# Two feed-forwards of a two-block network: up projections as seven block products instead of eight, down projections in one group per tile

## The reference

```python
def _swiglu(x, w1, w3, w2):
    return (jax.nn.silu(x @ w1) * (x @ w3)) @ w2
...
        x = _layernorm(DEEPNORM_ALPHA * x + 0.5 * _swiglu(x, ffn1_w1[l], ffn1_w3[l], ffn1_w2[l]),
                       ln1_g[l], ln1_b[l])
...
        x = _layernorm(DEEPNORM_ALPHA * x + 0.5 * _swiglu(x, ffn2_w1[l], ffn2_w3[l], ffn2_w2[l]),
                       ln3_g[l], ln3_b[l])
```

## Time and profile before

| | us |
|---|---|
| median of 3 runs | 3948.86 |
| lowest, highest | 3948.81, 3955.92 |
| profiled execution, span from first to last instruction | 3945.0 |
| TensorE busy | 3484.9 (88%) |
| VectorE busy | 1899.4 (48%) |
| ScalarE busy | 1151.9 (29%) |
| GpSimd busy | 80.0 (2%) |

### The profile page before, as it was taken

The page is one execution under the profiler, slowest core; times in us unless marked ns, Lnnn a source line. Parts: engine busy times, 40 slices in busy tenths (PEclk is TensorE's granted clock), DMA queues, the critical chain, the costliest instruction groups (busy, mean ns, idle before and its releaser), DMA issues. The chain is left out here.

```text
span 3945.0 us, 67598 instructions
## 1 busy us (share of the span) xinstructions
PE 3484.9 (88%) x30402; PEld 2794.9 (71%) x30402; DVE 1899.4 (48%) x2705; ACT 1151.9 (29%) x1713; POOL 80.0 (2%) x91
## 2 busy tenths in 40 slices
PE   2999899999757777779999999989967989999997
PEld 1888677887246767747888888767645768888885
DVE  7565455642656656446222222467785552222226
ACT  2111232222534334333211111235565331111113
POOL 0000000000000000000000000020000020000000
PEclk9999899999779999979999999999968999999999
DMA  4233311231741331142111111221000211111112
...
DMA packets 141692, 284.70 MB, mean 72 GB/s; under 512 B 8156, under 2 KB 81004, under 8 KB 141148
## 3 DMA queue, kind: packets, MB, share of 16 engines
...
...
## 5 line engine op out<-in xcount | busy, mean ns | idle before, releaser
L242 DVE TENSOR_TENSOR ring_b_wl<-ring_b_raw,ring_b_wh 128x1024 fp32r<-128x1024 f32 (+1 forms) x200 | 236.5, 1183 | 1112.9 <-ACT ring_b_wh L239 1112.9
L274 PE MATMUL PS<-ffn_x_high,ring_b_wh 128*128 128x512 f32 x1408 | 551.0, 391 | 13.1 <-DVE ffn_x_low L537 9.5
L239 ACT ACTIVATE ring_b_wh<-ring_b_raw 128x1024 fp32r<-128x1024 f32 (+1 forms) x200 | 204.6, 1024 | 1181.3 <-PE PS L276 1169.5
L276 PE MATMUL PS<-ffn_x_high,ring_b_wl 128*128 128x512 f32 x1408 | 549.2, 390 | 0.0
L275 PE MATMUL PS<-ffn_x_low,ring_b_wh 128*128 128x512 f32 x1408 | 549.0, 390 | 0.0
L274 PEld LDWEIGHTS PS<-ffn_x_high,ring_b_wh 128*128 128x128 f32 x1408 | 265.2, 188 | 73.8 <-issue 9.5
L276 PEld LDWEIGHTS PS<-ffn_x_high,ring_b_wl 128*128 128x128 f32 x1408 | 265.0, 188 | 55.3
L275 PEld LDWEIGHTS PS<-ffn_x_low,ring_b_wh 128*128 128x128 f32 x1408 | 265.2, 188 | 54.9 <-issue 0.2
L274 PE MATMUL PS<-ffn_hid_high,ring_b_wh 128*128 128x512 f32 x704 | 275.1, 391 | 2.6 <-DVE ring_b_wl L242 2.6
L276 PE MATMUL PS<-ffn_hid_high,ring_b_wl 128*128 128x512 f32 x704 | 273.9, 389 | 0.0
L275 PE MATMUL PS<-ffn_hid_low,ring_b_wh 128*128 128x512 f32 x704 | 273.9, 389 | 0.0
...
## 6 DMA issues: line engine op xcount, KB each, us to landing
...
```

What stands on the lines that cost most here:

```text
L239: return nc.scalar.activation(out, x, ACT.Copy)
L242: return nc.vector.tensor_tensor(out, x, high.bitcast(fp32), ALU.subtract)
L274: nc.tensor.matmul(out, wh, xh, start=k == 0, stop=False)
L276: last = nc.tensor.matmul(out, wl, xh, start=False, stop=k == kt - 1)
```

## The change

Only `ffn_stage` and the helpers it needs are rewritten. Hidden tiles 0 and 1 stay plain products (`plain`), 4 tiles x 2 token halves. For each hidden tile q = 2 to 21 (the code's quads), the two up tiles, each split into halves of k, form a 2x2 block matrix A (A11, A12 from w1, A21, A22 from w3), and `x` split by k and by tokens forms B (B11, B12, B21, B22). The four result blocks come of seven products of 4 blocks of k x 3 matmuls, on sums of blocks:

- On the weights, made by GpSimd for every q (`sums`): S1 = A21 + A22, S2 = S1 - A11, S3 = A11 - A21 (in place of A21), S4 = A12 - S2.
- On the data, made once: T1 and T2 by VectorE, T3 and T4 by GpSimd.
- The products in order: A11 B11, S2 T2, S1 T1, S3 T3, A12 B21, A22 T4, S4 B22. Each fills one of PSUM's banks 0 to 3. ScalarE copies the first to scratch; VectorE adds the others up in seven additions (`combine`), and two multiplications (`gate`) follow on ScalarE's two Silus, now from SBUF.

Both parts of every one of the seven operands are cut anew (128x512 each), into four slots of high parts and eleven slots that hold raw blocks, sums and, in place, their low parts. VectorE may overwrite A11 with its low part only after GpSimd's third sum, which still reads A11 (`SUMS_FOR`).

The down projection no longer sums over pieces. After the seven products of q all eight row tiles (down blocks) of hidden tile q - 2 follow: 6 matmuls each over 1024 tokens, in banks 4 and 5 or 6 and 7 by turns, and each added to `xT` at once by VectorE (`update`). A block may start when the update two before it is done. At q = 20 and 21 only the first token half is done so; the rest of it (hidden tiles 20 and 21 for the first half, 18 to 21 for the second) is left to the tail, in four single banks. The bias that `ffn2` adds to `xT` moves from GpSimd to ScalarE, as eight instructions of 128x1024 between the cuts of q = 2. Down weights come as one tile of a hidden tile's 1024 outputs.

```diff
-            PIECES = [(0, 8), (8, 8), (16, 6)]
-            tiles = []
-            for p, (first, n_hid) in enumerate(PIECES):
-                both = [("down", p, m, (0, 1)) for m in range(KD)]
-                if p == len(PIECES) - 1:
-                    both = [("down", p, m, (c,)) for c in range(2) for m in range(KD)]
-                tiles += [("up", p, m, (0, 1)) for m in range(2 * n_hid)] + both
...
+            KH = KD // 2
+            N_PLAIN = 2
+            QUADS = range(N_PLAIN, KF)
+            B11, B21, T1, T2, T3, T4, B22 = range(7)
+            PRODUCTS = (("A11", B11), ("S2", T2), ("S1", T1), ("S3", T3), ("A12", B21), ("A22", T4), ("S4", B22))
+            BANK_READ = ((-1, 2), (-1, 5), (-1, 6), (-1, 7), None, (0, 1), (0, 4))
+            PLACE = {w: i for i, (w, *_) in enumerate(PRODUCTS)}
+            ALLOC = ("A11", "S3", "A12", "A22", "S1", "S2", "S4")
+            BLOCKS = {"A11": (0, 0), "A12": (0, KH), "S3": (1, 0), "A22": (1, KH)}
+            SUMS_FOR = {"A11": 3, "S2": 4, "S1": 2, "S3": 3, "A12": 4, "A22": 1, "S4": 4}
...
+            BLOCKS_AFTER = {q: (0, 0, 0, 0, 0, 0, KD) for q in QUADS}
+            LOW_ORDER = (B11, B21, None, B22, T2, T1, T3, T4)
...
+                def await_slot(eng, q, w):
+                    j = allocation(q, w)
+                    if j >= N_SLOTS:
+                        was = j - N_SLOTS
+                        eng.wait_ge(prod.h, prod.base + number(N_PLAIN + was // 7, PLACE[ALLOC[was % 7]]) + 1)
+                    elif j >= 7:
+                        eng.wait_ge(prod.h, prod.base + 4 + (j - 7) // 2 + 1)
+                    elif j >= 3:
+                        eng.wait_ge(cut_low.h, cut_low.base + (j - 3) // 2 + 1)
...
+                        for q in range(4, KF):
+                            sp.wait_ge(blocks_done.h, blocks_done.base + block_count(q - 1))
+                            load_down(q - 2)
+                            load_quad(q)
...
+                        def sums(q):
+                            done = sums_done.base + 4 * (q - N_PLAIN)
+                            pool.wait_ge(raw_in[q % 2].h, raw_in[q % 2].base + 64 * ((q - N_PLAIN) // 2 + 1))
+                            a11, a12, a21, a22 = (slot(q, w) for w in ("A11", "A12", "S3", "A22"))
+                            s1, s2, s4 = (slot(q, w) for w in ("S1", "S2", "S4"))
+                            await_slot(pool, q, "S1")
+                            nc.gpsimd.tensor_tensor(s1, a21, a22, ALU.add).then_inc(sums_done.h, 1)
+                            await_slot(pool, q, "S2")
+                            pool.wait_ge(sums_done.h, done + 1)
+                            nc.gpsimd.tensor_tensor(s2, s1, a11, ALU.subtract).then_inc(sums_done.h, 1)
+                            nc.gpsimd.tensor_tensor(a21, a11, a21, ALU.subtract).then_inc(sums_done.h, 1)
+                            await_slot(pool, q, "S4")
+                            pool.wait_ge(sums_done.h, done + 2)
+                            nc.gpsimd.tensor_tensor(s4, a12, s2, ALU.subtract).then_inc(sums_done.h, 1)
...
+                            nc.gpsimd.tensor_tensor(row_source(T4, i), x_row(0, KH + i), row_source(T2, i), ALU.subtract)\
+                                .then_inc(t_pooled.h, 1)
...
+                        def product(q, i):
+                            w, o = PRODUCTS[i]
+                            n = number(q, i)
+                            pe.wait_ge(cut_low.h, cut_low.base + n - 4 * N_PLAIN + 3)
+                            if q == N_PLAIN:
+                                pe.wait_ge(x_low.h, x_low.base + rows_at(o) + KH)
+                            if i == 4:
+                                pe.wait_ge(copied.h, copied.base + q - N_PLAIN + 1)
+                            elif i < 4 and q == N_PLAIN:
+                                bank_read = multiplied if i % 2 else silu_done
+                                pe.wait_ge(bank_read.h, bank_read.base + i // 2 + 1)
+                            else:
+                                back, at = BANK_READ[i]
+                                pe.wait_ge(combined.h, combined_at(q + back, at))
+                            out, wh, wl = up_bank(q, i), highs[(n - 4 * N_PLAIN) % 4], rest(q, w)
+                            for k in range(KH):
+                                nc.tensor.matmul(out, wh[:, k, :], xh[:, o, k], start=k == 0, stop=False)
+                                nc.tensor.matmul(out, wh[:, k, :], xl[:, o, k], start=False, stop=False)
+                                last = nc.tensor.matmul(out, wl[:, k, :], xh[:, o, k], start=False, stop=k == KH - 1)
+                            last.then_inc(prod.h, 1)
...
+                        def down_block(q, m):
+                            u, n = q - 2, block_count(q) + m
+                            pe.wait_ge(down_low.h, down_low.base + u + 1)
+                            pe.wait_ge(hid_low.h, hid_low.base + max(4, gate_count(u, 1)))
+                            if n >= 2:
+                                pe.wait_ge(updated.h, updated.base + n - 1)
+                            else:
+                                pe.wait_ge(multiplied.h, multiplied.base + 4)
+                            out = block_banks(q, m)
+                            last = down([u], m, 0, out[:, 0:512])
+                            if q < FIRST_LATE + 2:
+                                last = down([u], m, 1, out[:, 512:1024])
+                            last.then_inc(blocks_done.h, 1)
...
+                        for q in QUADS:
+                            m = 0
+                            for i in range(7):
+                                product(q, i)
+                                for _ in range(BLOCKS_AFTER[q][i]):
+                                    down_block(q, m)
+                                    m += 1
...
+                        pe.wait_ge(down_low.h, down_low.base + KF)
+                        pe.wait_ge(hid_low.h, hid_low.base + gate_count(KF - 1, 1))
+                        pe.wait_ge(updated.h, updated.base + n0)
+                        for i in range(2 * KD):
+                            c, m = divmod(i, KD)
+                            if i >= 4:
+                                pe.wait_ge(updated.h, updated.base + n0 + i - 3)
+                            down(range(FIRST_LATE, KF) if c else range(KF - 2, KF), m, c, bank(TAIL_BANKS[i % 4]))\
+                                .then_inc(blocks_done.h, 1)
...
+                                if i == 0:
+                                    act.wait_ge(prod.h, prod.base + n + 1)
+                                    act.wait_ge(hid_low.h, hid_low.base + (gate_count(q - 1, 0) if q > N_PLAIN else 4))
+                                    nc.scalar.activation(unit(0), two(up_bank(q, 0)), ACT.Copy).then_inc(copied.h, 1)
+                                if i == 4:
+                                    act.wait_ge(combined.h, combined_at(q, 5))
+                                    nc.scalar.activation(unit(0), unit(0), ACT.Silu).then_inc(silu_done.h, 1)
+                                cut(n + 4)
+                                if q == N_PLAIN and i == 1 and biased_in:
+                                    act.wait_ge(x_low.h, x_low.base + 4 * len(LOW_ORDER))
+                                    for m in range(KD):
+                                        nc.scalar.activation(xT[:, m, 0:SEQ], xT[:, m, 0:SEQ], ACT.Identity,
+                                                             bias=head.bias(m, 0)).then_inc(biased_rows.h, 1)
+                                if i == 2 and q < KF - 1:
+                                    cut_down(q - 1)
+                                if i == 6:
+                                    act.wait_ge(combined.h, combined_at(q, 7))
+                                    nc.scalar.activation(unit(1), unit(1), ACT.Silu).then_inc(silu_done.h, 1)
+                                    act.wait_ge(blocks_done.h, blocks_done.base + block_count(q + 1))
+                                    hidden_high(q, 0, 0)
+                                    if q == KF - 2:
+                                        act.wait_ge(prod.h, prod.base + number(KF - 1, 0) + 1)
+                                    hidden_high(q, 1, 1)
...
+                                if i in (1, 3, 4, 5, 6):
+                                    dve.wait_ge(prod.h, prod.base + n + 1)
+                                if i == 1:
+                                    dve.wait_ge(copied.h, copied.base + q - N_PLAIN + 1)
+                                    dve.wait_ge(hid_low.h, hid_low.base + (gate_count(q - 1, 1) if q > N_PLAIN else 4))
+                                    combine(unit(1), unit(0), q, 1)
+                                elif i == 3:
+                                    dve.wait_ge(combined.h, combined_at(q, 1))
+                                    combine(unit(2), unit(1), q, 3)
+                                    dve.wait_ge(combined.h, combined_at(q, 2))
```

(20 more changed lines are left out.)

514 lines of the change are left out of this document (375 added, 139 removed).

## The result

| | before | changed |
|---|---|---|
| median, us | 3948.84 (4 runs) | 3975.11 (4 runs) |
| lowest, highest | 3942.8, 3955.92 | 3974.02, 3976.44 |
| ratio, 95% interval | | 1.0070 [1.0054, 1.0085] |
| span of the profiled execution | 3945.0 | 3974.0 |

The change costs 26 us where I forecast a gain of 21: 47 us off, and outside the range. 480 matmuls are gone (30402 to 29922), the clock stays at 1.00 behind the waits of every full q, and GpSimd's sum takes the 1.3 us that I took. What came out otherwise is how long VectorE's cuts take while GpSimd adds.

The account below looks back on a forecast made before the run. TensorE, busy throughout, bounds the kernel; fewer matmuls save 108.8 us. Gain with starts and ends is 87.1 - 36 s; at s = 1.84 it is 20.9, giving 3928 us (3915 to 3940, chance 0.42; whole range 3899 to 3968).

Parts of the forecast that it names:

- down cut 1.33: VectorE's cut of the down tile in each q, taken as 1.14 us plus 0.2 for GpSimd beside it.
- rival 3: VectorE held for GpSimd's whole S4 sum: 1.1 us more per q, loss 19, 3968; chance 0.20 together with rival 2.
- 1.84: TensorE's stall s per q in us: third down block 1.31 late, plus 0.53 for the fifth and seventh.
- tails: End of each feed-forward, VectorE setting its end: 43.7 us in all, of which 27.8 from the first second-half block.
- distance of 0.2267: TensorE's us between matmul starts, so each matmul saved is worth that if no other engine falls late.
- Rival 4: TensorE's clock falls to 0.50 in each q: 2 us each, 36 times, 72 in all, 4000; chance 0.05.
- p = 1.3: Time in us of one GpSimd weight sum, the middle of a copy's 0.90 and a one-scalar add's 1.78.
- Rivals 1 and 2: GpSimd quick, p 1.0 or less: gain 43 to 50, chance 0.20; sums decide, at 1.78: loss 13.7, 0.20 with rival 3.
- 4497 ns that I quoted: Skill page's GpSimd two-input add of 2048 columns; a quarter, about 1.2 us, would add 7 us to the gain; not used.
- First update: VectorE's first down update in each q, 21.7 us after the first matmul of the q's seven products.
- Start of `ffn2`: q = 2 starts at 3224.4; its seventh product 4.2 late, updates 4.3 later still; with half clock 11.5 us.
- wait before each tail: TensorE awaits last update, gate, two hidden cuts and two down cuts in turn: 5.85 us, half clock behind it.

Follow-up runs that it names:

- e1: Changed kernel with S4 not added, GpSimd only filling its slot with a constant (computation incomplete); 3929.52 us, 0.9968 of the kernel before.
- e5: The changed kernel again, no edit, beside the kernel before on the same chip; 3972.63 us, 1.0071 of the kernel before.
- e10: Changed kernel with T3 and T4 not made, GpSimd only filling their rows with a constant (computation incomplete); 3958.89 us, 1.0034 of the kernel before.
- e3: Changed kernel with one down block behind each product, two behind the last, instead of eight in one group; 3876.48 us, 0.9826 of the kernel before.
- e4: Changed kernel with none of the four weight sums added, GpSimd only filling their slots with a constant (computation incomplete); 3899.69 us, 0.9887 of the kernel before.
- e9: Changed kernel with GpSimd's order altered, S3 right behind S1, then S2 and S4; 3910.22 us, 0.9908 of the kernel before.
- e6: Changed kernel with one down block behind each product, two behind the last, and the down cut two products earlier; 3874.60 us, 0.9816 of the kernel before.

## Why the prediction was wrong

The step that failed is the term "down cut 1.33 (1.14 and 0.2 for GpSimd beside it)", part of the 7.8 us from the A11 cut to the first update. It measured 2.31. I knew the pair: it is rival 3, whose mechanism is right, and the hold is worth what it says (1.07 us a q in e1, for 1.1). Its total, 3968 for 3975, is near in part by luck: it puts the 1.1 on top of 1.84, 2.94 us a q where 2.65 were measured, and has the starts and tails too short. With the hold gone e1 waits 1.6 us a q, less than my 1.84, and takes 0.9968 of the kernel before: this one term turns a gain into a loss.

I took the short hold because of a row of 1.18 us and carried its excess of 0.4 over. That row is of another kind of GpSimd instruction (one tensor and one scalar per partition). GpSimd worked there without a break, around the whole of VectorE's instruction and of the next one like it:

```profile
3196.39 7.86 POOL L588 TENSOR_SCALAR xT<-xT,vec 128x512 f32<-128x512 f32 x4 [7.91 <-DVE ffn_x_low L537]
3200.98 1.17 DVE L499 SCALAR_TENSOR_TENSOR xT<-xT,vec,norm_std 128x512 f32<-128x512 f32 x1
```

So that kind holds VectorE for 0.4 us only; why it does stays open. For two additions or cuts of two tensors each, the runs show something else: the later one waits for what is left of the earlier, so the place matters. In my own timeline S4 was due at t = 13.9 together with the A11 cut, and the down cut at 14.5: if the A11 cut stops S4 until 14.5, the down cut waits for nearly all of S4.

The other terms, against the trace:

- Matmuls saved, distance of 0.2267, clock in a full q: right. Rival 4 is refuted: no wait of 1.8 us in the 34 full q's has half clock behind it. In q = 2 of `ffn1` one of 2.77 us has, for some 3.4 us (a window below), which is 1.7 of what that q took too much.
- GpSimd's sum, p = 1.3: measured 1.29 to 1.30. Rivals 1 and 2 fall with it. The A11 cut came at t = 13.8 (13.9). A quarter of the 4497 ns that I quoted is 1.12 us and not 1.2; by the prediction's sum that would have added 13 us to the gain and not 7.
- First update: t = 22.3 (21.7); third block 1.92 late (1.31); each later break 0.28 (0.26), and some 0.2 in smaller steps that I had left out. Waits in a full q 2.65 instead of 1.84, in 34 of them 28 of the 47 us. (Stalls of 66 us were six tenths of what the counts promise in the prediction's own sum, not half.)
- Start of `ffn2`: the same term again. I let T3 and T4 cost nothing beside VectorE; with the cuts they held, the start took 7.0 us more than forecast, q = 2 2.1 less. In `ffn1` q = 2 took 36.5 instead of 31.8 (34.9 in e5). Both starts with their q = 2 are 10 us over the forecast; e10 gives 11 to 12 us back there.
- The wait before each tail: 5.5 us (5.85), with 3.6 to 4.3 us of half clock behind it, as forecast. The tails took 46.2 and 48.8 instead of 43.7. In the middle of each TensorE waits 3.0 us for VectorE's sums for the norm (2577.45 and 3928.34); behind that wait the clock stays at 1.00 in the first tail and is at 0.50 for 5.6 us in the second, and half of that is about what the second takes more. The windows, columns as in the earlier trace rows: q = 2 of `ffn1`, then behind the wait before the first tail, behind the wait in it, and the same two for the second:

```profile
1924.20:1927.40 3.20, 3.16 (x8) 2.51 (x9) 1.25 (x2) 0.00 (x0) 0.00 (x0) 0.50 0.00 0
2548.40:2552.00 3.60, 3.60 (x9) 2.83 (x10) 0.67 (x1) 0.35 (x1) 0.00 (x0) 0.50 0.00 0
2577.50:2581.00 3.50, 3.50 (x14) 2.57 (x15) 2.48 (x4) 0.69 (x1) 0.00 (x0) 1.00 0.00 0
3899.50:3903.80 4.30, 4.30 (x10) 3.43 (x11) 1.11 (x2) 0.00 (x0) 0.00 (x0) 0.50 0.00 0
3928.40:3934.00 5.60, 5.60 (x11) 3.77 (x12) 2.47 (x4) 0.69 (x1) 0.00 (x0) 0.50 0.00 0
```

From first matmul to end `ffn1` is 22.5 us over the forecast and `ffn2` 26.1, on the traces' spans. Of these 49 us the full q's are 28, the starts with q = 2 10, q = 20 and 21 with the wait behind them 2.6, and the tails 7.6. The half clock in the second tail is 2.6 of those; the 2.5 that both have over the forecast stay open.

A second lack, not an error of size: I treated the waits of the group as given. e3 shows that they were a matter of order. A group of eight blocks asks for an update each 1.36 us right after VectorE's longest chain, and 1.22 us of update with 0.41 us of hand-over can't follow at that pace even if nothing is late (the 0.98 of e4 and e9). One block behind each product gives VectorE 4.08 us for each, and a down cut held to 2.04 us costs 0.1 us a q (e3 against e6). Whether more banks for the group would have done as well wasn't tried.
